# A fused PEER block and transformer layer on one core: the second half's rows turned unscaled, their norm rates applied where products come out

## The reference

```python
x = x + 0.5 * swiglu(rms_norm_2(x, g_f1), gate1, up1, down1)   # hidden width 2816
h = rms_norm_2(x, mix_norm)
proj = h @ w_in       # latents (352), fq, fk, fv (3 x 512), 8 forget logits, two gates (2 x 1024)
mixed = (sigmoid(g_mla + b0) * (y_mla @ w_branch_mla)
         + sigmoid(g_fox + b1) * (y_fox @ w_branch_fox))       # two causal attentions, 8 heads each
x = x + mixed @ w_o
x = x + 0.5 * swiglu(rms_norm_2(x, g_f2), gate2, up2, down2)
# rms_norm_2(x, g) = x * rsqrt(mean(x * x) + 1e-6) * g ; swiglu = (silu(x @ gate) * (x @ up)) @ down
```

## Time and profile before

| | us |
|---|---|
| median of 3 runs (2508.48 to 2516.59) | 2515.81 |
| the profiled execution, whole | 2518.81 |
| its span in the trace | 2517.0 |
| PE busy | 2120.6 (84%) |
| DVE busy | 1811.9 (72%) |
| ACT busy | 1184.0 (47%) |
| POOL busy | 762.0 (30%) |
| PE share of the chain that ended last | 42% |

### The profile page before, as it was taken

How to read it: one execution, slowest core, us unless ns; L and a number is a source line. 1 busy time by engine, 2 the same in 40 slices (tenths; PEclk the granted TensorE clock), 3 DMA queues, 4 the chain that set the end, 5 groups by cost and what they waited for, 6 DMA issues and landing times.

```text
span 2517.0 us, 28505 instructions
## 1 busy us (share of the span) xinstructions
PE 2120.6 (84%) x9496; PEld 1507.6 (60%) x9496; DVE 1811.9 (72%) x3316; ACT 1184.0 (47%) x3776; POOL 762.0 (30%) x634
## 2 busy tenths in 40 slices
PE   6987898988777778999665678699929989998999
PEld 6965443433222226874333565588429978797997
DVE  6985677768988887887898968666575545656554
ACT  5224565555666664442455644433244444445442
POOL 0001445454555543232555733333210001100000
PEclk9988999999999999999785789899959999899999
DMA  5111999999999999999998999999955542124453
GB/s 209 69 67 68 385 416 421 412 416 411 421 421 421 421 417 346 393 419 396 376 409 331 381 380 407 367 421 421 388 227 184 184 174 105 68 101 151 164 189 134
DMA packets 107458, 760.86 MB, mean 302 GB/s; under 512 B 12064, under 2 KB 12832, under 8 KB 16432
## 3 DMA queue, kind: packets, MB, share of 16 engines
q0 software_dynamic: 73728, 536.90, 52.4%
q1 hardware_dynamic: 33584, 222.15, 23.2%
HBM read 756.91 MB, written 2.10 MB: 302 GB/s over the span
## 4 chain that ended last, share of the span: by engine, by line
PE 42%; DVE 9%; DMA 4%; issue 3%; ACT 2%; POOL 1%; DVEq 0%; ACTq 0%; POOLq 0%
PE bank L566 41%; DMA pair<-in_uv,idx 4%; DVE resid L986 4%; DVE pair L1545 2%; DVE half L980 1%; ACT frow L1619 0%; DVE tmp L980 0%; PE bank L586 0%; PE bank L943 0%; POOL pair L2141 0%; ACT half L1619 0%; DVE smalls L1259 0%; POOL smalls L2096 0%; DVE ft_lo L980 0%; PE bank L823 0%
## 5 line engine op out<-in xcount | busy, mean ns | idle before, releaser
L2141 POOL DMA_INDIRECT pair<-in_uv,idx x512 | 652.0, 1274 | 875.2 <-DVE resid L986 558.3
L1619 ACT ACTIVATE smalls<-smalls 128x1 f32<-128x1 f32 x2058 | 540.6, 286 | 669.9 <-DVE smalls L1545 651.8
L1545 DVE CUSTOM_DVE_ANT_0 pair<-pair,hn 128x1024 f32<-128x1024 f32 x512 | 623.7, 1219 | 157.3 <-DMA pair<-in_uv,idx 155.7
L566 PE MATMUL bank<-pair,diag 128*128 128x512 f32 x928 | 454.1, 621 | 124.8 <-ACT diag L1619 124.2
L566 PEld LDWEIGHTS bank<-pair,diag 128*128 128x128 f32 x928 | 167.5, 193 | 393.8 <-ACT diag L1619 249.2
L566 PE MATMUL bank<-ft,raw 128*128 128x256 f32 x1664 | 373.6, 387 | 11.7 <-DVE ft L980 11.7
L986 DVE SCALAR_TENSOR_TENSOR resid<-pair,smalls,resid 128x1024 f32<-128x1024 f32 x280 | 358.0, 1279 | 0.6 <-ACT smalls L1619 0.3
L566 PEld LDWEIGHTS bank<-ft,raw 128*128 128x128 f32 x1664 | 323.4, 195 | 57.8 <-issue 12.4
L980 DVE TENSOR_TENSOR half<-raw,half 128x1024 fp32r<-128x1024 f32 (+1 forms) x204 | 235.0, 1194 | 114.0 <-ACT half L1619 114.0
L566 PE MATMUL bank<-ft_hi,half 128*128 128x256 f32 x1664 | 304.0, 284 | 7.5 <-DVE ft_lo L980 6.4
L1619 ACT ACTIVATE half<-raw 128x1024 fp32r<-128x1024 f32 (+1 forms) x204 | 199.6, 1029 | 146.2 <-PE bank L566 146.2
(11 more groups left out here) (262 smaller groups left out, 2620.8 us busy)
## 6 DMA issues: line engine op xcount, KB each, us to landing
raw<-in_wts SPq DMA_DIRECT2D x196, 1024.0 KB, 6.1
pair<-in_uv,idx POOLq DMA_INDIRECT x512
raw<-in_wts SPq DMA_DIRECT2D x10, 512.0 KB, 8.4
raw<-in_wts SPq DMA_DIRECT2D x4, 720.0 KB, 6.3
resid<-in_x SPq DMA_DIRECT2D x4, 512.0 KB, 6.6
out<-resid SPq DMA_DIRECT2D x8, 256.0 KB, 6.3
raw<-in_wts SPq DMA_DIRECT2D x2, 768.0 KB, 4.1
rowt<-in_rows SPq DMA_DIRECT2D x1, 1076.0 KB, 12.6
```

Source lines behind the costliest of these rows:

```text
L566: return e.matmul(o, a, b, start=start, stop=stop)
L1545: e.tensor_tensor_reduce(b[:, 0:1024], b[:, 0:1024], HN[i // 128], 1.0, 0.0, ALU.mult, ALU.add, actv[:, i % 8:i % 8 + 1]).then_inc(dotted, 1)
L1619: return e.activation(o, i, f, **kw)
L2141: e.indirect_dma_start(pair[i % NPAIR], None, uv, bass.IndirectOffsetOnAxis(ap=idx[:, n % SLOTS, k:k + 1], axis=0)).then_inc(pairs_in[i % ...
```

## The change

1. In B, PE turns the rows of `resid` themselves (`turned_unscaled`), without the rate. DVE gives them the gain (`turned_gained`), ACT rounds (`turned_first`), DVE makes the rest (`turned_rest`), tile by tile.
2. The rates follow separately. They are used as an ACT scale where `lat`, `fq`, `fk`, `fv` come out; as the scale of DVE's `add_tile` after the down products (`halved_rates`, `come_down`); and, where tokens lie along columns (up products, gates), as a 128x256 tile of rates: ACT writes two diagonals (`rates_spread`), PE multiplies them by ones (`rates_out`), ACT copies the bank (`rates_in`), and DVE multiplies by it (the gate half of each up chunk, now ahead of silu; `gate_scaled`, which replaces ACT's `gate_in`).
3. Tile 2 is turned, given its gain and rounded under the last rows of tile 3. Tile 3 is turned as soon as its last row is added: its final norm's gain is multiplied into the next one's (`g_fc`), its final rate into the next rate. The first weight chunk is rounded between rows 510 and 511.
4. `rows_times(..., by_tile=2)`: the last two pieces of the second half of "down" and of `wo`, and both of `lat`, are used for tile 2 first, then for tile 3.
5. The gates' sigmoids are 16 instructions of 256 columns instead of 3; the chunk `after(fqkv, 5)` is split ahead of attention instead of at its step 2; the first up chunk starts on its first split half.

The core of the diff (repeats for other stages left out):

```diff
+                order = [(m, i) for m in range(cut) for i in range(2)]
+                order += [(m, i) for i in range(2) for m in range(cut, len(pieces))]
...
+            def turned_unscaled(k, from_):
+
+                stage = "norm" + k if k[0] != "m" else "norm_" + k
+                for i in range(2):
+                    if from_ is not None:
+                        taken(e, from_, i)
+                        taken(e, from_, 2 + i)
+                    elif i == 0:
+                        e.wait_ge(x2_done, T0["B"] + 1)
+                    else:
+                        e.wait_ge(added, UP_TO[PAIRS][1])
...
+                    if c == 0 and p == "B":
+                        rates_out(str(f))
...
+                taken(e, f"rate{f}B", 0)
+                for c in range(22):
+                    o, _ = filled(e, up, c)
+                    tt(fsg[c % 4], o[:, 0:HALF], RATE[str(f)], ALU.mult).then_inc(h_scaled, 1)
+                    if c:
+                        multiplied(c - 1)
+                    if c > 1:
+                        hidden_rest(f, c - 2)
+                    split(after((f"f{f}", c, "B")))
...
+                    come_down(1, 1, 0)
+                    split(after(("d1", 10, p)))
+                    come_down(1, 1, 1)
+                    turned_gained("mB", 0, "g_m2", ntmp)
+                    turned_rest("mB", 0, ntmp)
+                    split(after(("d1", 11, p)))
...
+                    yield clock(508)
+                    mine()
+                    turned_gained("1B", 0, "g_f1", nearly)
+                    yield clock(510)
+                    turned_rest("1B", 0, nearly)
...
+            split(EARLY, (0,))
+            turned_gained("1B", 1, "g_fc", nearly)
+            turned_rest("1B", 1, nearly)
+            split(EARLY, (1,))
             final_mean(NT - 1)
             final_row(NT - 1)
-            split(EARLY)
-            split(EARLY + 1)
...
+                    if i == PAIRS - 2:
+                        row_used(e, PAIRS - 5)
+                        rounded(EARLY)
...
+                        for j in range(4):
+                            n = 8 - 8 * (c % 2) + 4 * (c // 2) + j
+                            taken(e, "gate" + p, n // 2)
+                            act(SIG[p][n], SIG[p][n], ACT.Sigmoid, bias=col("bg", n)).then_inc(sig_done, 1)
```

More of the change, by code:

```diff
@@ L194, in ffn @@
             p.ring(f"norm{f}{x}", 4, 1.5)
-            p.ring(f"up{f}{x}", 22, 7.0)
+            if x == "A":
+                p.ring(f"up{f}{x}", 22, 7.0)
+            else:
+                for stage, n in (("up", 1), ("rate", 1), ("up", 21)):
+                    p.ring(f"{stage}{f}{x}", n, 7.0)
             p.ring(f"down{f}{x}", 4, 19.0)
@@ L1008, in turned_out, with split @@
                     tt(dst[:, 1][sl], tv, dst[:, 0][sl].bitcast(F), ALU.subtract).then_inc(n_lo, 1)
-            def split(s):
+            def split(s, steps=(0, 1)):
                 if s is not None:
                     c = SPLITS[s]
-                    for m in range(2):
+                    for m in steps:
                         cut = slice(m * c.n // 2, (m + 1) * c.n // 2)
@@ L1340, in attention @@
                     prepared(p, n)
+                    if p == "B" and n == 2:
+                        gate_scaled(0)
+                    for c, at in GATE_AT[p].items():
+                        if n == at[1] + 1 and p == "B":
+                            gate_scaled(c)
                     if n in SPLIT_AT:
@@ L1427, in chain @@
                        ALU.mult).then_inc(out_, 1)
+                split(after(("fqkv", 5, p)))
                 yield from attention(p)
@@ L1892, in chain @@
                 yield from ffn(1, p, experts_done)
-                yield from normed("m" + p, p, ffn_done)
+                if p == "A":
+                    yield from normed("m" + p, p, ffn_done)
+                else:
+                    ffn_done(0)
+                    squared("mB", 0, resid[:, t0, :], frow[0])
+                    rounded(after(("d1", 10, p)))
+                    rounded(after(("d1", 11, p)))
+                    for i in range(2):
+                        turned_first("mB", i, ntmp)
+                    ffn_done(1)
+                    squared("mB", 1, resid[:, t0 + 1, :], frow[1])
                 rounded(after(("lat", 0, p)))
@@ L1925, in chain @@
                 yield from heads_in("fq", p)
+                if p == "B":
+                    rates_in("m")
                 rounded(after(("fqkv", 1, p)))
@@ L1960, in chain @@
                         act(MT2[0][:, n, :], SIG[p][n], ACT.Copy).then_inc(mt_hi, 1)
-                for q in range(4):
+                for q in range(2):
                     rounded(after(("wo", q, p)))
-                yield from ffn(2, p, mixers_done)
+                if p == "B":
+                    mixers_done(0)
+                    squared("2B", 0, resid[:, t0, :], frow[0])
+                    rounded(after(("wo", 2, p)))
+                    for i in range(2):
+                        turned_first("2B", i, ntmp)
+                    mixers_done(1)
+                    squared("2B", 1, resid[:, t0 + 1, :], frow[1])
+                    rounded(after(("wo", 3, p)))
+                    rates_spread("2B")
+                yield from ffn(2, p, mixers_done)
+                if p == "A":
+                    yield clock(505)
+                    experts_done(2)
+                    squared("1B", 0, resid[:, 2, :], frow[0])
+                    yield clock(509)
+                    turned_first("1B", 0, nearly)
             def scores_in_steps(c):
@@ L2096, in head_rate @@
                     e.tensor_tensor(sm8[(3 * j + 2) % 12], sm8[(3 * j + 1) % 12], mh[:], ALU.pow).then_inc(hn_rs, 1)
-                yield from rates("1" + p)
+                if p == "A":
+                    yield from rates("1" + p)
+                else:
+                    rate("1B", 1)
                 yield from rates("m" + p)
@@ L2110, in chain @@
                 yield from rates("2" + p)
+                if p == "A":
+                    yield clock(505)
+                    rate("1B", 0)
             rate("hn", 0)
```

303 lines of the change are left out of this document (214 added, 89 removed).

## The result

| | before, us | changed, us |
|---|---|---|
| median of 6 runs each | 2514.53 | 2491.80 |
| the profiled execution, whole | 2518.81 | 2490.55 |
| its span | 2517.0 | 2488.8 |
| row 505's dot to the last product, both traces | 677.17 | 651.24 |

The ratio of the runs is 0.9914 (95% interval 0.9894 to 0.9935): 22.7 us less by the medians, forecast 28.4. A second set of runs on one chip (experiment 11) gave 2492.76 (5 runs) against 2517.13 (9 runs), ratio 0.9906 (0.9892 to 0.9919). The two profiled executions lie 28.3 us apart, but 2.3 us of that lie ahead of row 505's dot (the eighth from the end, rows counted from 1), which was issued at 1836.63 and at 1834.29. In the fourteen profiles of this document it came anywhere from 1831.7 to 1839.0 us, so those 2.3 us are chance.

The account below looks back on a forecast made before the run. PE was taken to bound the second half, working nearly without a break, with time and clock lost at the joints. Terms summed to -28.4 us, taking the median from 2515.8 to 2487.4 us, range 2477.5 to 2503.

Parts of the forecast that it names:

- rows' end, row 505's dot to up: Last rows to the first up product: last addition 2.2 us later, up products at 1867.0 instead of 1877.27, -10.3 us.
- after the first FFN, to `fq`: Last down product to first `fq` product: 14.35 us instead of 22.27, the clock staying full, -7.9 us.
- attention: Attention's start: PE's 3.7 us wait shrinks by 1.6 and the clock stays, worth 4.5 of 6.6 us; together -6.1.
- branches and `wo`, with sigmoids: Branch products through `wo`: +0.9 us for sixteen sigmoids at 0.36 each, +0.8 for the second piece's split inside `wo`.
- `wo` to the second FFN: Last `wo` product to first up product: 6.05 us instead of 12.35, the clock falling as before.
- rates on PE: Three times two products and a bank, 0.2 us each, one under a wait: +0.5 us, to +1.
- up and down stages: Both FFNs: the up stage keeps its pace, 5.65 us of PE for a chunk; no cost counted.
- The rival of the stretched rows' loop: Rows' loop: added steps upset the last gathers, at most a few us, total 2491; chance 0.06.
- my first rival: Clock falls anyway at attention's start, perhaps after the first FFN too; gain 23.9 or 21.2, 2491.9 to 2494.6; chance 0.22.
- the prediction's own signs of being wrong: Silus' spacing grows, last addition moves by over 4 us, or PE waits over 1 to 2 us for joints' weight splits.
- The rival that the up stage becomes DVE and ACT's: 44 up chunks: to eat the 28.4 us each must take 0.65 us more; with 2 us longer line, 2533; chance 0.03.
- rival 2: DVE's order eats the three joints, each losing 3 to 4 us: gain 17 to 19, total about 2498; chance 0.22.

Follow-up runs that it names:

- experiment 11: The changed kernel run again unedited, on one chip with the kernel before: median 2492.76 us over 5 runs, ratio 0.9906 to the kernel before.
- experiment 12: The kernel before the change, run again unedited for a second profile: 2516.37 us.
- Experiment 2: Changed kernel with tile 2's square, mean, gain, rounding and rest moved behind the last row's addition, its turning on PE still early: 2489.37 us.
- experiment 3: Changed kernel with the weight split for `after(fqkv, 5)` put back into attention, where it stood before the change: 2502.18 us.
- experiment 4: Changed kernel with five needless copies of the first probability block added on DVE ahead of the real one: 2501.82 us.
- experiment 7: Changed kernel with filler products of constants on PE, 48 under the last rows' additions, 16 behind the last turning, 34 behind `wo`: 2500.42 us.
- experiment 1: Changed kernel with all of `by_tile` undone, so the last pieces serve both tiles piece by piece as before the change: one execution, 2499.98 us.

## Why the prediction was right

The forecast was 2487.4 us (2477.5 to 2503), the medians 2491.8 and 2492.8. The profiled execution was forecast at 2490.4 and took 2490.55, but by 2.3 us of luck ahead of the change. Term by term, forecast and measured (differences of the table's first and third rows; for stretches that aren't in it, of the same two traces):

| term | forecast | measured |
|---|---|---|
| rows' end, row 505's dot to up | -10.3 | -11.0 |
| after the first FFN, to `fq` | -7.9 | -7.6 |
| attention | -6.1 | -7.6 |
| branches and `wo`, with sigmoids | +1.7 | +2.9 |
| `wo` to the second FFN | -6.3 | -6.4 |
| rates on PE | +0.5 | +0.2 ahead of `fk`, 0.9 in the next row |
| up and down stages | 0 | +3.5 |
| sum | -28.4 | -25.9 |

- **Rows' end.** Right in size and in steps: the gap was 4.2 us (4.2 forecast), and the last addition came 1.5 us (2.7 in experiment 11 against 12) later, where 2.2 was forecast. By experiments 11 and 12 the term is -9.7. Experiment 2 shows that this delay eats most of what the early work saves. The rival of the stretched rows' loop did not show: DVE waited for no gather in the last three rows.
- **After the first FFN.** 4.66 and 14.71 us against 4.55 and 14.35, with a wait of 1.62 against 1.5. The step from wait to clock was luck in part: I had argued from one 1.0 us gap that the clock would stay, and in experiments 3, 4 and 7 it fell there for 3.4 us, worth 1.3 us.
- **Attention.** The wait of 2.0 us was right. The clock's gain was taken at 4.5 of 6.6 us (the stretch of the earlier trace rows, by finer windows 13.7 us and not 13.3, makes it 6.8); where the clock costs nothing it was 6.0 (7.6 less 1.65 for the wait). That the clock stays was half right: in five of the seven profiles with this code at attention's start it fell ahead of the wait and cost nothing, in experiment 7 it stayed, and in experiment 1 it was lost. When it falls, as in experiment 1, the term is -2.7 (135.01 against 137.72). That was my first rival, and it is the same code there on another execution, not another outcome of the change. It may be part of the changed kernel's spread of 11 us in the first set of runs; the kernel before spreads as widely, so that isn't shown.
- **Sigmoids, the mis-sized term.** I took 0.36 us each from copies of 256 columns. They take 494 ns and follow each other every 0.41 (6.51 us for 16):

```profile
L1780 ACT ACTIVATE sigB<-sigB,colt x16: 492/494/508, 2243.3 to 2249.3; 128x256 f32<-128x256 f32 x16
```

  So they cost 2.7 us more than three did, ACT's saving of 0.7 came before, and PE's wait grew from 0.42 to 1.92 us: +1.5 where +0.9 stood. The Trainium skill (ScalarE: Activation LUTs, What ACT_TABLE_LOAD costs) states 280 ns plus 0.833 a column for an activation with a bias column, an estimate of 493 ns for 256 columns, and an overlap of 93 ns; the trace agrees, and I hadn't used it. The +0.8 us of tile order inside `wo` was right (0.81). The stage grew by 0.6 us beyond these two; 0.2 of that lies between the two profiles of the kernel before (40.11 and 40.34), the rest I didn't trace.
- **The up stages.** "Keeps its pace" was wrong by 0.7%: 5.695 against 5.653 us, 1.9 us over both. A grown spacing of the silus was one of the prediction's own signs of being wrong; 0.04 us a chunk is far from the 0.65 that its rival needed. Of the other 1.1 us of the two, 0.9 are the rates' products and 0.2 a longer low clock under the first chunk (5.6 us instead of 5.3). The down stages took 0.24 to 0.27 more; in experiment 12 the kernel before took 62.84 and 62.82 too, so that is no cost of the change. The rival that the up stage becomes DVE and ACT's did not show: no chunk waited.
- **Rates on PE, mis-sized too.** Two products were priced at 0.2 us. They are four instructions, and in each FFN the products behind them come 0.45 us later.
- **Order at the joints** (rival 2) cost nothing: the three gaps are within 0.4 us of the walk.
- **Small readings.** The clock line shows one digit of 8 in the second half, and not a dip for each joint; the joints' low clock is in the earlier trace rows. The best bounds add up to -37.8 us, which is 2478.0 and not 2477.5.

## What to carry to other kernels

A factor that only scales rows or columns can be put in behind the product; what it saves is the latency of the line that makes it (here square, mean, rate, scaled rows), not engine time. With the new order of the steps around it that was 6 to 11 us at each joint; how much is the order's alone isn't shown, except for the tile order's 3.2 us over two joints (one execution). When such a joint is walked instruction by instruction with durations of the trace, gaps come out within half a us; what went wrong was a unit price taken from a neighbour of another form (a copy for a sigmoid with a bias, one instruction for an f32 product that is two) and a pace taken as fixed. And a wait of PE costs its length plus, by chance, half of a low stretch of the clock behind it, so a forecast should carry the clock as two outcomes of one kernel, and fillers that fit the wait can buy the better one.

## What the runs showed of the hardware

- Low stretches of the granted clock that began in the second half were 3.4, 6.8, 10.2 or 13.6 us long (read within 0.2 us) in all profiles, whatever the wait ahead of them (0.6 to 5.5 us). In the kernel before it was low for 13.7 us at attention's start although PE had no idle time from 2148.5 to 2162.4 us.
- An f32 product of 128x128 by 128 columns is two instructions, 0.22 us together at full clock (68 instructions in 7.8 us in experiment 7); a turning of the same size is one, 0.11 (8 after the first FFN take 1.06 us, the last one's 0.27 whole).
- PE ran at the same granted clock 0.7% slower per product in the changed kernel's up stages than in the old one's, in every profile of either. PE waited for nothing there, and the cause wasn't found.
